# Modulation rows on four column groups of the array, their partial sums added by a selection matmul

## The reference, cut to what matters

```
shift, scale, gate = split((silu(c) @ w_mod + b_mod), 3)
shift_c, scale_c, gate_c = split(silu(c_ctx) @ w_mod + b_mod, 3)
h  = rms_norm(x,   norm_w) * (1 + scale)   + shift
hc = rms_norm(ctx, norm_w) * (1 + scale_c) + shift_c
...
x_new = x + gate * merge_branches(...)
```

## Time and profile before

| what | value |
|---|---|
| median of 3 runs | 2233.93 us (2231.27 to 2236.58) |
| profiled execution, first to last instruction | 2233.1 us |
| around the span, against the median | 0.8 us |
| PE busy | 2155.3 us, 97% |
| TensorE clock granted, mean | 0.991 |
| bytes moved | 218.29 MB, mean 98 GB/s |

### The profile page before, as it was taken

How to read it: one execution, slowest core, us unless ns; L and a number is a source line. 1 busy time by engine, 2 the same in 40 slices (tenths; PEclk the granted TensorE clock), 3 DMA queues, 4 the chain that set the end, 5 groups by cost and what they waited for, 6 DMA issues and landing times.

```text
span 2233.1 us, 28302 instructions
## 1 busy us (share of the span) xinstructions
PE 2155.3 (97%) x12000; PEld 1683.8 (75%) x12000; DVE 982.5 (44%) x1762; ACT 633.1 (28%) x1085; POOL 143.8 (6%) x181
## 2 busy tenths in 40 slices
PE   7999999999999999999999999999999999999997
PEld 2248888887788888888888888888873345888886
DVE  1334334554245555545554565362245333454333
ACT  3222321232322222322223212542244332222121
POOL 0000000000011111100011001100000002010000
PEclk9999999999999999999999999999999999999999
DMA  8752112222221111211111211444322332444332
GB/s 305 275 199 66 57 57 62 67 89 62 67 75 58 48 57 58 67 49 57 57 48 58 65 53 54 130 143 130 104 76 89 109 132 94 151 145 176 121 114 85
DMA packets 151927, 218.29 MB, mean 98 GB/s; under 512 B 9632, under 2 KB 99993, under 8 KB 150521
## 3 DMA queue, kind: packets, MB, share of 16 engines
q1 hardware_dynamic: 136777, 173.08, 24.8%
q0 software_dynamic: 7248, 29.25, 3.8%
q10 hardware_dynamic: 7776, 14.16, 1.8%
HBM read 198.11 MB, written 18.35 MB: 97 GB/s over the span
## 4 chain that ended last, share of the span: by engine, by line
PE 87%; DVE 4%; ACT 4%; DMA 2%; issue 1%; POOL 0%; SPq 0%; ACTq 0%; POOLq 0%; DVEq 0%
PE psum L1324 20%; PE psum L1326 20%; PE psum L1325 20%; PE psum L1410 6%; PE psum L1377 4%; PE psum L1375 3%; PE psum L1557 2%; ACT inv L601 1%; PE psum L1387 1%; PE psum L1385 1%; PE psum L1352 1%; DMA w_raw<-w_mod_dram 1%; PE psum L1393 1%; ACT square_out L633 1%; DVE inv L929 1%
## 5 line engine op out<-in xcount | busy, mean ns | idle before, releaser
L845 DVE TENSOR_TENSOR w_lo<-w_raw,w_hi 128x1024 fp32r<-128x1024 f32 (+1 forms) x233 | 284.9, 1223 | 654.2 <-ACT w_hi L535 653.9
L535 ACT ACTIVATE w_hi<-w_raw 128x1024 fp32r<-128x1024 f32 (+1 forms) x233 | 246.3, 1057 | 1129.4 <-PE psum L1326 1101.7
L1324 PE MATMUL psum<-h_hi,w_hi 128*128 128x512 f32 (+1 forms) x1168 | 486.4, 416 | 5.7 <-DVE w_lo L845 3.5
L1325 PE MATMUL psum<-h_lo,w_hi 128*128 128x512 f32 (+1 forms) x1168 | 461.3, 395 | 0.0
L1326 PE MATMUL psum<-h_hi,w_lo 128*128 128x512 f32 (+1 forms) x1168 | 461.0, 395 | 0.0
L1326 PEld LDWEIGHTS psum<-h_hi,w_lo 128*128 128x128 f32 (+1 forms) x1168 | 220.4, 189 | 50.9
L1324 PEld LDWEIGHTS psum<-h_hi,w_hi 128*128 128x128 f32 (+1 forms) x1168 | 220.8, 189 | 44.4 <-DVE w_lo L845 4.9
L1325 PEld LDWEIGHTS psum<-h_lo,w_hi 128*128 128x128 f32 (+1 forms) x1168 | 221.3, 189 | 33.7
L1410 PE MATMUL psum<-w_raw_mod,silu_c 128*2 128x512 f32 x256 | 114.0, 600 | 1.3 <-ACT silu_c L660 0.8
L1375 PEld LDWEIGHTS psum<-invT,L 128*128 128x128 f32 x768 | 93.6, 192 | 22.0 <-DVE inv L929 19.0
L1375 PE MATMUL psum<-invT,L 128*128 128x64 f32 x768 | 95.3, 274 | 12.3 <-DVE inv L929 11.4
(11 more groups left out here) (293 smaller groups left out, 3106.8 us busy)
## 6 DMA issues: line engine op xcount, KB each, us to landing
w_raw<-w_in_dram SPq DMA_DIRECT2D x168, 512.0 KB, 3.6
w_raw_mod<-w_mod_dram SPq DMA_DIRECT2D x64, 512.0 KB, 4.8
w_raw<-w_mod_dram SPq DMA_DIRECT2D x32, 512.0 KB, 3.9
w_raw<-w_out_dram SPq DMA_DIRECT2D x32, 512.0 KB, 3.7
gate_scratch<-gate_stage ACTq DMA_DIRECT2D x48, 256.0 KB, 3.2
gates<-gate_scratch POOLq DMA_DIRECT2D x32, 256.0 KB, 4.0
w_raw<-w_proj_a_dram SPq DMA_DIRECT2D x16, 512.0 KB, 3.6
w_raw<-w_proj_b_dram SPq DMA_DIRECT2D x16, 512.0 KB, 3.6
```

Source lines behind the costliest of these rows:

```text
L535: act.activation(part(whi[i % 2], p), part(place, p), ACT.Copy).then_inc(S("w_hi"), 1)
L845: dve.tensor_tensor(part(wlo[i % 2], p), part(raw_of(n)[0], p), part(whi[i % 2], p).bitcast(f32), ALU.subtract).then_inc(S("w_lo"), 1)
L1324: pe.matmul(out_ap, lh, rh, start=first, stop=False, skip_group_check=shared)
L1325: pe.matmul(out_ap, lh, rl, start=False, stop=False, skip_group_check=shared)
```

## The change

Each k-tile's product is now written to one of four places in the bank: partitions 0, 32, 64 or 96, by k modulo 4 (and so by one of the four groups of 32 columns of the array). Each of the four accumulates every fourth k-tile. Since the other partitions of the bank are read too, DVE clears banks 4, 5 and 7 once. ACT copies all 128 partitions of the bank, and the transposes are replaced by matmuls against a new constant `SEL`, 128 x 8, with a one where the partition modulo 32 is the column's number; its first two columns add the four partial sums while they turn rows into columns. SP's loads, buffers, semaphores and the order of the work on each engine stay.

```diff
+SEL = STAGE + len(MASKED) * 2 * 64
+NCONST = SEL + 8
...
+    parts.append(t % 32 == np.arange(8)[None, :])
...
-    mrow = at("mod_rows", [2, 512], A_T + 9728)
+    mrow = at("mod_rows", [P, 512], A_T + 9728)
...
-                act.activation(mrow_g[:], bank(7)[0:2], ACT.Copy).then_inc(S("modg_rows"), 1)
+                act.activation(mrow_g[:], bank(7), ACT.Copy).then_inc(S("modg_rows"), 1)
...
-                        act.activation(mrow[:], bank(4 + gi % 2)[0:2], ACT.Copy).then_inc(S("mod_rows"), 1)
+                        act.activation(mrow[:], bank(4 + gi % 2), ACT.Copy).then_inc(S("mod_rows"), 1)
...
+            for b in (4, 5):
+                dve.memset(bank(b), 0.0).then_inc(S("rows_zero"), 1)
             dve.wait_ge(S("const_in"), 16)
...
+            dve.wait_ge(S("kt_evac"), KV)
+            dve.memset(bank(7), 0.0).then_inc(S("rows_zero"), 1)
             att_max(0)
...
-                    ins = pe.transpose(bank(b, 2, 2 * q), rows_t[:, q * P:(q + 1) * P], ident[0:2, 0:2])
+                    ins = pe.matmul(bank(b, 2, 2 * q), rows_t[:, q * P:(q + 1) * P], consts[:, SEL:SEL + 2], start=True, stop=True)
...
+                    if kind == "mod" and first and gi < 2:
+                        pe.wait_ge(S("rows_zero"), gi + 1)
+                    if gi == MODGS[0] and first:
+                        pe.wait_ge(S("rows_zero"), 3)
                     for kk in range(p["nk"]):
-                        ins = pe.matmul(bank(b0)[0:2], sc2[:, p["k0"] + kk, :], part3(place, p)[:, kk, :],
-                                        start=first and kk == 0, stop=last and kk == p["nk"] - 1)
+                        k = p["k0"] + kk
+                        c0 = 32 * (k % 4)
+                        ins = pe.matmul(bank(b0)[c0:c0 + 2], sc2[:, k, :], part3(place, p)[:, kk, :],
+                                        start=k < 4, stop=k >= KT - 4)
```

More of the change, by code:

```diff
@@ L33 @@
 MASKED = BLOCKS[:-2]
-NCONST = STAGE + len(MASKED) * 2 * 64
+SEL = STAGE + len(MASKED) * 2 * 64
+NCONST = SEL + 8
 def shape_constants():
@@ L267, in build @@
     kvr = at("kv_rows", [P, NT, 512], A_C + 16384)
-    mrow_g = at("mod_gate_rows", [2, 512], A_T + 8192)
+    mrow_g = at("mod_gate_rows", [P, 512], A_T + 8192)
     sqj = at("square_out", [P, P], A_T + 12288)
```

## The result

The changed kernel takes 2221.66 us (median of 8 runs, 2215.86 to 2230.46) against 2237.2 for the kernel before in the same session (8 runs): a ratio of 0.9932, 95% interval 0.9910 to 0.9954. It is faster, by some 15 us, where 40 were forecast; the time lies outside the range. The profiled execution has a span of 2213.8 us, 19.3 less than before; it is the fastest of the eight, so the stages read from it add up to more than the 15 us between the medians.

What follows compares the result with a forecast made beforehand. PE was taken as the bound, busy 97% of the span, with loads held by its products. From 2233.1 us, 27 off the `mod` stage and 13 off attention gave 2193.1, plus 0.8 makes 2194; range 2184 to 2212.

Steps and rivals of the forecast that it cites:

- Side by side: Both weight stages: a piece's two products run beside each other, 0.86 us of streaming plus 0.16 of tail, 1.02 us.
- strictly in order: Rival, both stages: products start only in program order, a piece is released after 1.45 us; 2205 us, chance 0.22.
- no overlap: Rival, both stages: groups sharing rows take turns; 2241 us, or 2272 if group changes drain the array; chance 0.09.
- Term 1, the `mod` stage: Stage at the start: loads at 388 GB/s instead of 288, 7 us of gaps, 27 us sooner (22 to 31).
- the 14 places that I counted: `mod` stage: six token transposes and eight groups' ends, where the load queue runs dry, 5 us together.
- The added work: Groups' ends in the `mod` stage: 4.6 us more of PE, costing nothing beside transfers, 4.6 us if uncovered.
- Term 2, the attention: Attention: eight runs of four pieces win 2.5 us each, 20 us, less deductions 13 us (8 to 17).
- the 5.8 that I took off before the clock: Attention deductions: 3 us for the first eight steps, 2.3 for groups' ends, 0.5 for clearing bank 7.
- one more stretch at 1.2 GHz: Attention: PE idles more often, so one further slow-clock stretch was allowed for, 0.9 us.
- Between the stages: Between first projection product and first scores: what follows the first stage moves as a block, forecast change 0.
- The sum: Whole kernel: span 2233.1 - 27 - 13 = 2193.1 us, plus 0.8 around it, median 2194.
- The rival "the clock": Attention: idle PE lowers the clock to 1.2 GHz, ten stretches take all the gain; 2207 us, chance 0.07 (with another floor).

Runs made afterwards that it cites:

- e5: Changed kernel with eight instead of four weight buffers in the `mod` stage at the start: 2199.36 us, ratio 0.9837 to the kernel before.
- e1: Changed kernel with all products back in one column group, the added clears, copies and selection matmuls kept: 2247.96 us, ratio 1.0051 to the kernel before.
- f1_filler_mod: Changed kernel, four buffers, with an added product of zeros behind each group's first six pieces in the `mod` stage: 2219.16 us, ratio 0.9909.
- f3: Changed kernel with eight buffers at the start, six in attention, and added products of zeros in both places: 2188.77 us, ratio 0.9780.
- e8: Kernel before, products in one group, given eight buffers at the start and six in attention: 2231.15 us, ratio 0.9977.
- e2: Changed kernel with column groups only in the `mod` stage at the start, one group in attention: 2228.65 us, ratio 0.9970.

## Why the prediction was wrong

*Side by side.* Right. A piece takes 1.03 us; 1.02 were forecast for its release. The step from separate tiles to shared rows held. The rivals "strictly in order" and "no overlap" are out: the second start comes within 0.03 us of the first, where the halves of one product are 0.43 us apart, so the second k-tile starts before the first one's second half, and the piece takes 1.03 us and not 1.45. The Trainium skill, "TensorE: Matmul & The Clock Gate", Part 3, What overlaps and what doesn't, says that matmuls start strictly in program order. By the starts above the trace disagrees for products that share all rows, too. The same page of the Trainium skill, section "Measured speedup vs the span model", puts packed tiles about 4 ns apart. The rows above agree in kind: two starts within 0.03 us, and eight instructions of 0.59 us each in 1.04 us.

*Term 1, the `mod` stage: the step that failed.* It was "a buffer is away for 1.02 us of products, 0.1 for the semaphore and the 3.9 us from issue to landing, 5.0 us in all, so the queue just stays filled". The 3.9 us was that of the attention, where at most two loads are under way. In the stage it is 5.5, and 5.0 from 80 to 118 us, where the clock is full and no tokens are loaded:

```profile
w_raw_mod<-w_mod_dram SPq DMA_DIRECT2D x24, 512.0 KB, 5.0
```

So a buffer is away for 6.1 to 6.6 us where the four hold 5.4 us of transfers. The queue then runs dry between pieces, not only at the 14 places that I counted: four pieces in 6.1 us are some 340 GB/s, and 338 were measured in that stretch. A load's time includes its standing behind other loads, so it alone would not show the cause; the eight buffers of e5 do, with which a load takes longer still (9.7 us) and the rate is 385 GB/s. The page of before has 4.8 us for these very transfers, which would already have given 5.9 against 5.4; I took the wrong row of the two. The gaps that I put at 7 us are 117.5 - 37.8 MB / 388 GB/s = 20 us. The rest of this term was sound: with eight buffers the same stage moves its 38.0 MB at 385 GB/s and wins 32.5 us, more than the forecast 27.

*The added work.* "Beside transfers that set the pace, so nothing" presumed a full queue. In the open it costs some 4 us in the stage (e1, without its later start and its stretch at 1.2 GHz), against 4.6 named for that case. With eight buffers it is hidden, as forecast. How much of it shows with four isn't known.

*Term 2, the attention.* Right in mechanism, too large in size: 8.8 us were won instead of 13, at the low end of its own bounds. From the first piece's start to the last one's end the eight runs of four won 15.0 us together instead of 20; what was lost beside them, 6.2, is near the 5.8 that I took off before the clock. The term that was too small is the clock: one more stretch at 1.2 GHz, 0.9 us, was allowed for, and the profile has 27.3 us of them instead of 3.4. Two runs of two, one and one pieces, which last 13.97 and 13.96 us before, show its price. In the changed kernel they won 0.1 and 0.9 us, at a granted clock of 0.75 and 0.87; in `f1_filler_mod`, with the same instructions in the attention, 2.7 and 2.6 at full clock (columns as in the earlier trace rows, first after, then f1):

```profile
1754.54:1768.38 13.84, 10.41 (x42) 4.70 (x42) 5.97 (x12) 4.50 (x8) 0.54 (x1) 0.75 0.40 133
1799.58:1812.63 13.05, 9.51 (x42) 4.32 (x42) 5.84 (x11) 4.50 (x8) 4.78 (x9) 0.87 0.66 204
```

```profile
1756.59:1767.86 11.27, 7.89 (x42) 3.40 (x42) 5.84 (x11) 4.50 (x8) 0.54 (x1) 1.00 0.51 163
1800.76:1812.10 11.34, 7.89 (x42) 3.38 (x41) 5.84 (x11) 4.50 (x8) 4.78 (x9) 1.00 0.67 224
```

These two alone are 4.3 us, as much as the term misses. The whole attention of f1 is no shorter all the same (182.1 us), since its 20.5 us of half-clock time lie in other places; no profile with four groups has an attention without it. Where fillers and buffers together took most of the waits and some of the half-clock time away (f3), the attention is 16.5 us shorter than before.

*Between the stages.* The code is the same, and I forecast nothing; 2.9 us were lost. Over the 14 profiles of this case the length of this part goes with its half-clock time: 1514 us plus 0.47 us for each us at half clock (correlation 0.98). The shortest of them, e1, had 6.8 us of it, the longest but two, e5, had 37.5:

```profile
153.20:1671.40 1518.20, 1491.66 (x9479) 1278.45 (x9479) 723.10 (x1339) 435.95 (x778) 97.61 (x95) 1.00 0.25 71
```

```profile
113.50:1645.20 1531.70, 1505.55 (x9478) 1289.47 (x9479) 722.86 (x1339) 436.19 (x778) 97.65 (x95) 0.99 0.25 71
```

Before and after have 27.3 us each, so the clock does not explain the 2.9 us. The two profiles without the change, before and e8, lie 2.1 and 2.0 us below that line, the other twelve between 0.7 below and 1.5 above it: the change seems to make this part some 2 us slower, and why stays open.

*The sum.* The span is 20.7 us above the forecast one (2193.1): 13.3 from the stage at the start, 4.2 from the attention, 2.9 from between them, 0.3 from the end. The median lies 28 us above the forecast: in its session the kernel before took 2237.2 us, not the 2233.9 from which I counted, and the profiled execution is the fastest. The rival "the clock" had the place right, the attention, but not the price, some 4 us and not 13; and that the stage at the start bears a lower clock for nothing is doubtful (e2).

## What to carry to other kernels

When a faster engine hands the pace to the transfers, count the ring anew: the time from issue to landing in that very queue at that depth, plus the use, against what the buffers hold; a ring that "just" holds runs dry at each disturbance. A change that makes products cheaper and a change that adds buffers may each win little and win together what neither shows alone (here 0.7% and 0.2% apart, 1.8% with both). And where PE is given idle time, look in the rows for half-clock time in the stages that it still sets.

## What the runs showed of the hardware

- Products on all 128 rows and different column groups start within 0.03 us of each other; four k-tiles (eight instructions) take 1.04 us, two take 1.03, four on two groups 1.89.
- With eight buffers one 0.5 MB load took longer from issue to landing (9.7 us median instead of 5.5) and the rate rose from 322 to 385 GB/s. A longer time of one load is thus no sign of slower transfers.
- The same run of pieces in the attention took 11.27 us at a granted clock of 1.00 and 13.84 at 0.75.
- In 27 executions of the kernel before in one session, the mean granted clock lay between 0.988 and 0.993 and the time between 2244 and 2231 us, some 2 us for each 0.001. The eight of the changed kernel lie at 0.974 to 0.982.
